# Two norms in a row: VectorE sums into h, and GpSimd makes the low parts

## The reference

```python
y = swiglu(y, ffn1_w_gate[l], ffn1_w_up[l], ffn1_w_down[l])
h = h + FFN_RESIDUAL_WEIGHT * g1 * rmsnorm(y, ffn1_post_g[l])
y = rmsnorm(h, mix_pre_g[l]) * (1.0 + sc2) + sh2
y = token_mix(y, w_in[l], ...)
h = h + g2 * rmsnorm(y, mix_post_g[l])
y = rmsnorm(h, ffn2_pre_g[l]) * (1.0 + sc3) + sh3
y = swiglu(y, ffn2_w_gate[l], ffn2_w_up[l], ffn2_w_down[l])
h = h + FFN_RESIDUAL_WEIGHT * g3 * rmsnorm(y, ffn2_post_g[l])
```

## Time and profile before

| | us |
|---|---|
| median of 3 runs | 2256.31 |
| lowest and highest | 2254.43, 2256.95 |
| the profiled execution | 2255.29 |
| its span, first to last instruction | 2253.4 |
| TensorE busy | 2219.3 (98%) |
| VectorE busy | 1312.9 (58%) |
| ScalarE busy | 848.0 (38%) |
| GpSimd busy | 246.1 (11%) |

### The profile page before, as it was taken

One profiled execution on the slowest core, in us unless ns is written; L12 is line 12 of the kernel. 1 busy time (PEld: TensorE's weight loads), 2 busy tenths in 40 slices (PEclk: granted clock), 3 DMA queues, 4 the chain that ended last, 5 costly groups with the idle time before them and its releaser, 6 DMA issues.

```text
span 2253.4 us, 30747 instructions
## 1 busy us (share of the span) xinstructions
PE 2219.3 (98%) x12700; PEld 1814.7 (81%) x12700; DVE 1312.9 (58%) x1967; ACT 848.0 (38%) x1318; POOL 246.1 (11%) x193
## 2 busy tenths in 40 slices
PE   8999999999999999999999999999999999999998
PEld 6888888778777888887788888888887779888887
DVE  6755547668268455547633576665387776644443
ACT  4322224544544323223633443323255554423221
POOL 0000003104023000003110100000134321000001
PEclk9999999999999999999999999999999999999999
DMA  7766632222122366542231246664132113533221
GB/s 305 251 214 218 211 126 93 99 80 67 47 65 69 128 215 206 187 131 87 79 105 57 66 161 216 205 214 149 64 108 66 38 56 105 176 105 100 95 95 38
DMA packets 82362, 287.22 MB, mean 127 GB/s; under 512 B 9136, under 2 KB 12080, under 8 KB 81712
## 3 DMA queue, kind: packets, MB, share of 16 engines
q1 hardware_dynamic: 81360, 283.43, 37.8%
q10 hardware_dynamic: 864, 1.84, 0.2%
HBM read 283.13 MB, written 2.10 MB: 127 GB/s over the span
## 4 chain that ended last, share of the span: by engine, by line
PE 88%; DVE 8%; ACT 1%; issue 1%; DMA 0%; POOL 0%; SPq 0%; DVEq 0%; ACTq 0%
PE bank L308 24%; PE bank L310 24%; PE bank L309 24%; DVE wlo L1785 2%; PE bank L451 1%; PE bank L452 1%; PE bank L453 1%; DVE tmps L2005 1%; PE bank L1016 1%; PE bank L477 1%; PE bank L1032 1%; PE bank L364 1%; PE bank L472 1%; PE bank L358 1%; PE bank L780 1%
## 5 line engine op out<-in xcount | busy, mean ns | idle before, releaser
L308 PE MATMUL bank<-yhi,whi 128*128 128x512 f32 (+1 forms) x1670 | 653.1, 391 | 0.2 <-DVE ylo L2151 0.2
L310 PE MATMUL bank<-yhi,wlo 128*128 128x512 f32 (+1 forms) x1670 | 644.6, 386 | 0.0
L309 PE MATMUL bank<-ylo,whi 128*128 128x512 f32 (+1 forms) x1670 | 644.5, 386 | 0.0
L1785 DVE TENSOR_TENSOR wlo<-raw,whi 128x1024 fp32r<-128x1024 f32 (+2 forms) x373 | 470.4, 1263 | 266.7 <-ACT whi L1130 266.1
L1130 ACT ACTIVATE whi<-raw 128x1024 fp32r<-128x1024 f32 (+2 forms) x373 | 383.7, 1031 | 291.9 <-PE bank L310 247.3
L308 PEld LDWEIGHTS bank<-yhi,whi 128*128 128x128 f32 x1670 | 314.1, 188 | 79.0 <-issue 15.8
L310 PEld LDWEIGHTS bank<-yhi,wlo 128*128 128x128 f32 x1670 | 314.0, 188 | 63.9
L309 PEld LDWEIGHTS bank<-ylo,whi 128*128 128x128 f32 x1670 | 314.3, 188 | 60.5 <-issue 0.2
L308 PE MATMUL bank<-mlp_ahi,whi 128*128 128x512 f32 (+1 forms) x552 | 206.6, 374 | 0.0
L309 PE MATMUL bank<-mlp_alo,whi 128*128 128x512 f32 (+1 forms) x552 | 206.2, 374 | 0.0
L310 PE MATMUL bank<-mlp_ahi,wlo 128*128 128x512 f32 (+1 forms) x552 | 206.2, 374 | 0.0
(11 more groups left out here) (386 smaller groups left out, 2703.2 us busy)
## 6 DMA issues: line engine op xcount, KB each, us to landing
raw<-in_ada SPq DMA_DIRECT2D x152, 512.0 KB, 4.3
raw<-in_ffn_up SPq DMA_DIRECT2D x88, 512.0 KB, 4.3
raw<-in_mlp_up SPq DMA_DIRECT2D x64, 512.0 KB, 3.3
raw<-in_mlp_dn SPq DMA_DIRECT2D x64, 512.0 KB, 3.3
raw<-in_ffn_dn SPq DMA_DIRECT2D x32, 512.0 KB, 3.7
raw<-in_w_dqkv SPq DMA_DIRECT2D x24, 512.0 KB, 3.3
raw<-in_ffn_dn SPq DMA_DIRECT2D x16, 384.0 KB, 3.6
first<-in_ada SPq DMA_DIRECT2D x8, 512.0 KB, 16.8
```

Of the source, the lines that this page charges most:

```text
L308: e.matmul(out, wh, xh, start=first, stop=False)
L309: e.matmul(out, wh, xl, start=False, stop=False)
L310: mm = e.matmul(out, wl, xh, start=False, stop=last)
L1785: e.tensor_tensor(k.wlo[:, home, at:at + width], raw[:, 0:width], k.f(k.whi[:, home, at:at + width]), ALU.subtract).then_inc(*sig.up("wlo" ...
```

## The change

In all three bridges VectorE makes every sum itself, right behind its post, and then scales the same tile. It no longer makes the low parts. ScalarE makes yhi(n) and directly behind it the whole shifted tile, now for ffn2 too. GpSimd subtracts yhi(n) from that whole tile to get ylo(n) (signal "plo", for which TensorE now waits), and no longer makes sums. The memsets of GpSimd wait for yhi 0 in place of ylo 0 and stand behind the last subtraction. VectorE's weight remainder stands behind scaled 2.

```diff
@@ Act.prenorm
         def whole(n):
 
-            w.wait_ge(*sig.on("ylo", st, n))
             self.e.activation(k.tm(n)[:, 0:S], k.tm(n)[:, 0:S], k.ACT.Identity,
                               bias=k.mod[:, 8 * v_shift + n:8 * v_shift + n + 1]).then_inc(*sig.up("yfull", st, n))
...
-            if st != "ffn2" and n > 1:
-                whole(n - 2)
-        if st != "ffn2":
-            whole(6)
-            whole(7)
+            whole(n)
@@ Dve.bridge
         def scaled(n):
-            w.wait_ge(*sig.on("hp" if n else "hv", st, n))
+            w.wait_ge(*sig.on("hv", st, n))
...
-        def low(n):
-            w.wait_ge(*sig.on("yhi", nx, n))
-            e.scalar_tensor_tensor(k.ylo[:, n, :], k.tm(n)[:, 0:S], k.mod[:, 8 * v_shift + n:8 * v_shift + n + 1],
-                                   k.f(k.yhi[:, n, :]), ALU.add, ALU.subtract).then_inc(*sig.up("ylo", nx, n))
+        def summed(n):
+            w.wait_ge(*sig.on("post", st, n))
+            e.tensor_tensor(k.h[:, n, :], k.h[:, n, :], k.tm(n)[:, 0:S], ALU.add).then_inc(*sig.up("hv", st, n))
 
         w.wait_ge(*sig.on("spread", "R", st))
         post(0)
         self.root(st + "h")
-        w.wait_ge(*sig.on("post", st, 0))
-        e.tensor_tensor(k.h[:, 0, :], k.h[:, 0, :], k.tm(0)[:, 0:S], ALU.add).then_inc(*sig.up("hv", st, 0))
-        post(1)
+        summed(0)
         scaled(0)
-        post(2)
         for n in range(1, NT):
+            post(n)
+            summed(n)
             scaled(n)
-            if n == 1:
-                low(0)
-                post(3)
-                continue
-            low(n - 1)
             if n == 2:
                 self.prep_to(self.u + NW - 1)
-            if n + 2 < NT:
-                post(n + 2)
-        low(7)
@@ Pool.bridge
-        for n in range(1, NT):
-            w.wait_ge(*sig.on("post", st, n))
-            self.e.tensor_tensor(k.h[:, n, :], k.h[:, n, :], k.tm(n)[:, 0:S], ALU.add).then_inc(*sig.up("hp", st, n))
+        for n in range(NT):
+            w.wait_ge(*sig.on("yfull", nx, n))
+            self.e.tensor_tensor(k.ylo[:, n, :], k.tm(n)[:, 0:S], k.f(k.yhi[:, n, :]), ALU.subtract).then_inc(
+                *sig.up("plo", nx, n))
@@ Pool.program
-        w.wait_ge(*sig.on("ylo", "mix", 0))
+        w.wait_ge(*sig.on("yhi", "mix", 0))
         e.memset(k.attd["mix"][:, :, :, :], 0.0)
```

More of the change, by code:

```diff
@@ L639, in ffn @@
         k = self.k
-        y = (k.yhi, k.ylo, "ylo", (st,))
+        y = (k.yhi, k.ylo, "plo" if st == "ffn2" else "ylo", (st,))
         def up(g):
@@ L785, in mix @@
         w, sig, e, k = self.w, self.sig, self.e, self.k
-        y = (k.yhi, k.ylo, "ylo", ("mix",))
+        y = (k.yhi, k.ylo, "plo", ("mix",))
         self.four(["hq"] * 4, y, "yhi", 3, 2)
@@ L907, in gla @@
         w, sig, e, k = self.w, self.sig, self.e, self.k
-        y = (k.yhi, k.ylo, "ylo", ("gla",))
+        y = (k.yhi, k.ylo, "plo", ("gla",))
         self.four(["gq"] * 4, y, "yhi", 3, 2)
@@ L2606, in squares, with bridge @@
                                      ALU.add).then_inc(*sig.up("sqadd", st, n, t))
-    def bridge(self, st):
+    def bridge(self, st, nx):
         k, w, sig, ALU = self.k, self.w, self.sig, self.k.ALU
@@ L2645, in program @@
         k, w, sig, e, ALU = self.k, self.w, self.sig, self.e, self.k.ALU
-        self.bridge("ffn1")
-        w.wait_ge(*sig.on("ylo", "mix", 0))
+        self.bridge("ffn1", "mix")
+        w.wait_ge(*sig.on("yhi", "mix", 0))
         e.memset(k.attd["mix"][:, :, :, :], 0.0)
@@ L2660, in program @@
             e.tensor_tensor(k.mo[:, h, :], k.mo[:, h, :], k.mqk[:, h, :], ALU.mult).then_inc(*sig.up("gmo", h))
-        self.bridge("mix")
-        self.bridge("ffn2")
-        w.wait_ge(*sig.on("ylo", "gla", 0))
+        self.bridge("mix", "ffn2")
+        self.bridge("ffn2", "gla")
+        w.wait_ge(*sig.on("yhi", "gla", 0))
         e.memset(k.attd["gla"][:, :, :, :], 0.0).then_inc(*sig.up("attz", "gla"))
```

## The result

The changed kernel takes 2259.03 us, the median of 20 runs (2257.31 to 2260.51); the kernel before, on the same chip, takes 2255.47 us, the median of 20 runs (2254.41 to 2257.01). The ratio is 1.0016 with an interval of 1.0009 to 1.0023, so the change costs 2.0 to 5.2 us. That is inside the range and inside the bound of 0.2% called no difference, and slower beyond doubt all the same. The forecast was 1.7 us over the kernel before; the medians stand 3.6 apart, so the loss is twice the one that was forecast.

What follows compares the result with a forecast made beforehand. TensorE holds 88% of the chain, and each bridge is decided by when yhi(3) is there. Losses of 0.37, 0.61 and 0.73 us, together 1.7, on the median of 2256.31 gave 2258.0 us; range 2254.2 to 2262.0.

Steps and rivals of the forecast that it cites:

- What bounds the bridge: At each bridge: the time yhi(3) is there decides; TensorE's wait for it grows from 1.1 to about 1.5 us.
- The exclusion rule and its tails: VectorE operations with two SBUF inputs and GpSimd's exclude each other; the second comer then runs 0.55, 1.15 or 1.08 us.
- The chain from scaled(0) to tile 3: In each bridge, TensorE resumes 9.99 us behind scaled(0) instead of 9.15: 0.84 more.
- The head start of scaled(0): At the bridges' start, scaled(0) no longer follows post(1): 0.47, 0.23 and 0.11 us earlier in the three bridges.
- Edits at no cost: Behind and beside the bridges: moved memsets, earlier freed raw slot and whole tiles for ffn2 cost nothing.
- An undelayed remainder: Rival, in the bridges: GpSimd's low(1) doesn't hold up the weight remainder; a gain of 0.7 us, 2255.6; chance 0.12.
- a slow subtraction: Rival, in the bridges: GpSimd's subtraction takes 1.74 to 2.0 us, pushing scaled(3); 2260.9 to 2262.5; chance 0.14.
- The rival's mechanism: Rival, behind tile 3's wait: TensorE's clock falls, losing 1.7 us in each bridge, + 5.1, 2263.1; chance 0.08.

Runs made afterwards that it cites:

- new_again: The changed kernel unaltered, run once more for a second timing and profile; 2259.69 us against 2255.54 for the kernel before (1.0018).
- new_third: The changed kernel unaltered, run for a third profile; its single run gives 2258.09 us.
- new_long: The changed kernel with GpSimd's subtractions of tiles 0 to 6 longer by 192 columns, each also waiting for the one before; 2263.62 us against 2255.85 (1.0036).
- new_gp: The changed kernel with each bridge's one weight remainder made by GpSimd in two halves ahead of its subtractions; 2254.24 us against 2255.54 (0.9996).

## Why the prediction was right, and where its sizes were off

The forecast of 2258.0 was 1.0 under the measured 2259.03, and its sign was right. That it came so near is in part luck: it was added to a median of 2256.31 from three runs, and that of 20 is 2255.47, so 0.8 of the missing 1.9 us were made up by the base. The change itself was put at 1.7 and measured at 3.6. By its steps:

What bounds the bridge. Right: it is yhi(3). TensorE waits 1.36 there in all three bridges. The text expected the wait to grow from 1.1 to about 1.5; its level was read too high (the kernel before waits 0.94 there, "0.9" in the row above), its growth of 0.4 is right.

The exclusion rule and its tails. Right to the hundredth: 1.08, 1.15 and 0.55 as above, each taken from a row of the kernel before. The remainder was forecast at 1.74 (399.75 to 401.49) and took 1.74; the third sum was forecast at 1.01 and took 1.01; the other sums take 0.69 and the subtraction 1.29 to 1.30, forecast 1.28. The Trainium skill's rule ("SBUF — State Buffer", section "Who interferes with whom") was thus worth following; this case's rows agree with it for every remainder, sum and subtraction shown above, down to an operation of 8 columns.

The chain from scaled(0) to tile 3. Forecast +0.84 in each bridge, measured +0.88 (10.03, 10.04, 10.03).

The head start of scaled(0). Here the sizes failed. The text had it start 0.03 behind the end of the spread root and took that end from the kernel before: 0.47, 0.23 and 0.11 earlier, 0.81 together. Counted from post(0), scaled(0) starts 2.05 behind it in the old order and 1.68 in the new one: 0.36 to 0.37 earlier in the first bridge. There the releaser is now TensorE's last matmul on the root's bank (0.21 of idle time in the row above), and scaled(0) starts 1.68 behind post(0) where the text had 1.58. In the second bridge nothing is gained; scaled(0) comes 2.14, 2.15 and 2.26 behind post(0) in the three profiles of the new order, 0.1 to 0.2 later than in the old, because the last of TensorE's four root matmuls stands for 0.30 to 0.41 with "issue" named, where it stands for at most 0.15 in the three profiles of the kernel before. The timelines of TensorE and VectorE in the second bridge of after, against the earlier trace rows, where the four are one row of 0.90:

```profile
699.61 0.27 PE L626 MATMUL bank<-cst,rs 128*128 128x128 f32 x1 [0.30 <-issue]
...
700.02 0.75 DVE L2049 SCALAR_TENSOR_TENSOR tmps<-h_sb,coef,bank 128x512 f32<-128x512 f32 x1 [0.67 <-PE bank L626]
```

In the third bridge it is 1.69 in new_again and new_third, so 0.36, and 2.15 in the first profile, whose low clock stretched the root. The text read that bridge's 0.11 off a profile whose clock was low as well; it is a figure of that execution, not of the bridge. Put right, the sum is 0.88 - 0.36, 0.88 + 0.12 and 0.88 - 0.36, together 2.0 us; the table above has 0.51, 1.0 and, of the undisturbed pair, 0.5. So the step that was mis-sized is the head start: 0.81 us in the sum, 0.60 measured (0.36, -0.12 and 0.36).

Edits at no cost. The stretches behind the bridges are unchanged (274.64 and 274.67, 1157.9 and 1157.9), so the moved memsets, the freed raw slot and the whole tiles for ffn2 cost nothing that a trace shows.

The rivals. An undelayed remainder did not come; a slow subtraction did not come either, but new_long shows what it would have done, at 1.20 instead of 0.96. A low clock behind the stop in front of the third bridge appears in three profiles of 14, in both orders; it is a risk of the kernel, not of the change. Behind the wait for tile 3 the clock is at 1.00 in all three profiles of the changed kernel, at a wait of 1.4, as forecast. The rival's mechanism is real all the same: in new_long, at a wait of 2.25, the clock fell in two bridges of three, and cost 1.44 us in the first, where the rival had put 1.7.

What stays open. The terms above make 2.0 us, the three profiled executions of each order stand 2.4 us apart in their spans and 2.7 in their times, and the timed medians 3.6 in the first comparison and 4.2 in that of new_again. Two things can be read from the other executions. The time holds something outside the span that the prediction took as unchanged: 2.1 us in the changed kernel and 1.9 in the one before, alike in every comparison, so 0.2 us of the loss lie outside the span; why is not shown. And the median span of the timed executions is 2257.6 against 2253.7 in the comparison of new_again, 3.9 apart, while the changed kernel's three profiles have 2256.8, 2255.8 and 2256.0: they lie in the lower part of its executions. Both intervals of the timed comparisons hold 2.7, so the rest of about 1 us may be no more than scatter; if it is a loss, no profile here shows its place. The third bridge with its stop scatters most, but that it carries the rest is argued and not shown.

## What to carry to other kernels

When work is handed from one engine to another, list for each moment which operations of VectorE with two SBUF tiles (and which TENSOR_SCALARs) and which of GpSimd are pending: the second comer stands until the first is done, and a long one that is fitted between (here a weight remainder of 1.1 us) is passed on as a chain of delays to the step that TensorE waits for. Put the long operation where GpSimd is idle and VectorE is not in a hurry, or give it to GpSimd behind the last small operation that the critical path needs, in pieces that end before the next one: here this moved the version from 3.6 us slower to 2.6 us faster, though in the third bridge, where that last operation came at another moment, the pieces fell on the sum. A head start is worth what its releaser allows, so read that releaser in more than one execution before it goes into a sum.

## What the runs showed of the hardware beyond this

The size of the waiting operation doesn't matter: one of 4 columns is held until GpSimd is done, like one of 512. What size decides is how long it runs behind that: its undisturbed time less 0.14 us. A VectorE add of 0.69 ends 0.55 behind GpSimd, a remainder of 1.22 ends 1.08 behind it, a GpSimd operation of 1.29 ends 1.15 behind VectorE's, and the one of 4 columns here, 0.15 undisturbed, ends with GpSimd (412.40 + 0.68 against 411.77 + 1.29). Behind the first bridge of after, VectorE meets GpSimd's subtraction and then its memset (both engines, in order of time):

```profile
411.77 1.29 POOL L2604 TENSOR_TENSOR ylo<-tmps,yhi 128x512 fp32r<-128x512 f32 x1 [0.86 <-ACT tmps L1264]
412.40 0.68 DVE L2183 TENSOR_TENSOR lbc<-par 128x4 f32<-128x4 f32 x1
...
415.16 1.81 POOL L2634 MEMSET attd<- 128x2048 f32 x1
...
415.82 0.16 DVE L2192 TENSOR_TENSOR lbc<-lbc 128x4 f32<-128x4 f32 x1
416.02 0.97 DVE L2194 TENSOR_SCALAR lbc<-lbc 128x4 f32<-128x4 f32 x1
```

In the kernel before the first of them takes 0.15 and a larger operation runs beside the memset:

```profile
411.97 1.82 POOL L2648 MEMSET attd<- 128x2048 f32 x1
...
413.16 1.62 DVE L2059 SCALAR_TENSOR_TENSOR ylo<-tmps,mod,yhi 128x512 fp32r<-128x512 f32 x2
```

The small TENSOR_SCALAR at 416.02, with one tile to read, ends with the memset at 416.99, and in new_gp another took 1.14 behind GpSimd's subtraction: so it is held up with one SBUF input as well, by a memset and by a subtraction, while post and scaled, with an operand in PSUM, are never held up in any row here. Operations that read two tiles pass a memset undisturbed: the TENSOR_TENSOR at 415.82 took 0.16 beside the one of after, and low(6), at 413.16 beside the one of the kernel before, took 0.74. So the two kinds differ in these rows: two tiles to read are held up by a GpSimd operation that reads, TENSOR_SCALAR by either. No run was made to tell the reason.

TensorE's wait for an instruction ahead of the third bridge falls on the 74th of 96 matmuls of one burst (73 ahead of it, x23 behind it in the row above) in every profile, but lasts from 1.3 to 2.2 us. A difference of 1 us between two single profiles that lies there says nothing of the kernels.
